# A hybrid HGRN2 / retention layer step: query pads inside the value stage, one gate moved across a round's border, two small groups of matmuls in 64-column tiles

## What is computed

```
xn = RMSNorm(h); hq, hf, hi, hg, rq, rk, rv, rg, ga, gb = split(xn @ w_in)
# branch A: 8 heads, state 64x64, chunk by chunk
f = lb + (1 - lb) * sigmoid(hf)
S_t = diag(f_t) S_{t-1} + (1 - f_t) i_t^T ;  o_t = S_t^T silu(q_t)
a_hg = head_rmsnorm(o_hg) * silu(hg)
# branch B: 4 heads of 128, rotary q and k, decay gamma_h
a_r = head_rmsnorm(retention(q_r, k_r, rv)) * silu(rg)
mixed = sigmoid(ga) * (a_hg @ w_br_hg) + sigmoid(gb) * (a_r @ w_br_ret)
h = h + mixed @ w_out ; h = h + ConvFFN(RMSNorm(h)) ; h = h + ple gate ; y = RMSNorm(h)
```

## Time and profile before

| what | value |
|---|---|
| median of 3 runs | 937.52 us (937.37 to 937.79) |
| the profiled execution, its own time | 936.62 us |
| its span, first to last instruction | 934.8 us |
| PE busy | 911.3 us, 97% of the span |
| DVE, ACT, POOL busy | 56%, 42%, 25% |
| granted TensorE clock | 0.995 |

### The profile page before, as it was taken

The page is one execution under the profiler, slowest core; times in us unless marked ns, Lnnn a source line. Parts: engine busy times, 40 slices in busy tenths (PEclk is TensorE's granted clock), DMA queues, the critical chain, the costliest instruction groups (busy, mean ns, idle before and its releaser), DMA issues. The chain is left out here.

```text
span 934.8 us, 20997 instructions
## 1 busy us (share of the span) xinstructions
PE 911.3 (97%) x7950; PEld 896.8 (96%) x7950; DVE 523.9 (56%) x613; ACT 388.7 (42%) x518; POOL 236.0 (25%) x289
## 2 busy tenths in 40 slices
PE   6999999999999999999999999999999999999996
PEld 5999988999999999999999999999999999999995
DVE  6432267777655655566566655555556433435653
ACT  7323356446345544323344444444443322213433
POOL 0006076777211010002631111111111021212341
PEclk9999999999999999999999999999999999999998
DMA  6333533233254434633323333333333333332212
GB/s 223 93 91 90 180 92 80 79 90 79 79 137 112 127 97 135 199 117 99 90 68 91 90 90 90 91 90 94 94 94 105 102 93 93 93 90 70 81 54 91
DMA packets 176471, 94.72 MB, mean 101 GB/s; under 512 B 17888, under 2 KB 174960, under 8 KB 176016
## 3 DMA queue, kind: packets, MB, share of 16 engines
q1 hardware_dynamic: 149698, 80.61, 29.0%
q10 hardware_dynamic: 26736, 13.60, 5.5%
HBM read 86.25 MB, written 8.03 MB: 101 GB/s over the span
## 5 line engine op out<-in xcount | busy, mean ns | idle before, releaser
L832 ACT ACTIVATE whi<-raw 128x1024 fp32r<-128x1024 f32 (+2 forms) x132 | 146.9, 1113 | 351.0 <-PE acc L486 350.2
L1169 DVE TENSOR_TENSOR wlo<-raw,whi 128x1024 fp32r<-128x1024 f32 (+2 forms) x132 | 195.7, 1482 | 172.3 <-ACT whi L832 172.3
L486 PE MATMUL acc<-xah,whi 128*128 128x260 f32 x896 | 186.9, 290 | 0.0
L486 PE MATMUL acc<-xah,wlo 128*128 128x260 f32 x896 | 180.2, 283 | 0.0
L486 PE MATMUL acc<-xal,whi 128*128 128x260 f32 x896 | 179.7, 282 | 0.0
L486 PE MATMUL acc<-xbh,whi 128*128 128x260 f32 x816 | 165.3, 284 | 0.8 <-issue 0.8
L486 PE MATMUL acc<-xbh,wlo 128*128 128x260 f32 x816 | 164.4, 283 | 0.0
L486 PE MATMUL acc<-xbl,whi 128*128 128x260 f32 x816 | 164.2, 283 | 0.0
L486 PEld LDWEIGHTS acc<-xah,whi 128*128 128x128 f32 x896 | 137.9, 189 | 3.3 <-issue 1.9
L486 PEld LDWEIGHTS acc<-xal,whi 128*128 128x128 f32 x896 | 137.9, 188 | 0.0
L486 PEld LDWEIGHTS acc<-xah,wlo 128*128 128x128 f32 x896 | 137.8, 188 | 0.0
(11 more groups left out here) (287 smaller groups left out, 1183.4 us busy)
## 6 DMA issues: line engine op xcount, KB each, us to landing
raw<-in_w_in SPq DMA_DIRECT2D x96, 256.0 KB, 3.1
raw<-in_w_up SPq DMA_DIRECT2D x88, 256.0 KB, 3.1
raw<-in_w_down SPq DMA_DIRECT2D x16, 384.0 KB, 3.3
raw<-in_w_down SPq DMA_DIRECT2D x16, 320.0 KB, 3.7
raw<-in_w_out SPq DMA_DIRECT2D x16, 256.0 KB, 3.0
raw<-in_w_ple_gate SPq DMA_DIRECT2D x8, 512.0 KB, 3.8
x_transposed<-xstg SPq DMA_DIRECT2D x1, 2080.0 KB, 7.5
hT<-x_transposed ACTq DMA_DIRECT2D x1, 2080.0 KB, 7.9
```

The lines of the kernel that those rows point to most:

```text
L486: mm = pe.matmul(sums[:, b, 0:HT], wt[slot][:, w], xx[:, c, b * HT:(b + 1) * HT], start=first and i == 0 and q == 0, stop=last and i == n ...
L832: act.activation(whi[k % 2][:, 0:n], raw[k % 2][:, 0:n], ACT.Copy).then_inc(hi_ready, 1)
L1169: dve.tensor_tensor(wlo[k % 2][:, 0:n], raw[k % 2][:, 0:n], whi[k % 2][:, 0:n].bitcast(fp), SUB).then_inc(lo_ready, 1)
```

## The change

Six edits. (1) ACT's loop over section V is written out, and the pads of the levels 0 to 3 of the first round are made inside its second half, two levels after each of the first two units. (2) At the end of a B round ACT makes `branch_hi` before the sigmoid. (3) DVE makes the gate `grt` of a round not at its end but in the next round, between `merge(0)` and `merge(1)`; for this the first round is written out ahead of the loop, and the last gate stands behind it. (4) L578 and L691 become twice as many matmuls of 64 weight columns, one for each half of the output partitions. (5) In a C round the copy and the squares of the samples' outputs stand ahead of the low weight part. (6) The small sums of squares stand behind four chunks instead of five.

```diff
--- before.py
+++ after.py
@@ -575,7 +575,9 @@
                 taken()
                 if use == 3:
                     for c in range(4):
-                        pe.matmul(lvb[:, 1, 2 * c:2 + 2 * c], qk[:, c, :], headsel, start=True, stop=True)
+                        for r in range(2):
+                            rows = slice(64 * r, 64 * r + 64)
+                            pe.matmul(lvb[rows, 1, 2 * c:2 + 2 * c], qk[:, c, rows], headsel, start=True, stop=True)
                 for l in levels:
                     for c in range(4):
                         out = lvb[:, l % 2, c * 128:(c + 1) * 128].rearrange("s (two t) -> s two t", two=2)
@@ -688,16 +690,18 @@
                 pe.wait_ge(smp_staged, it + 5)
                 pe.wait_ge(rsm_ready, it + 1)
                 for b in range(NS):
-                    mm = pe.matmul(mb[:, b:b + 1], rsm[:, b, :], qs8[:, b:b + 1], start=True, stop=True)
+                    for r in range(2):
+                        rows = slice(64 * r, 64 * r + 64)
+                        mm = pe.matmul(mb[rows, b:b + 1], rsm[:, b, rows], qs8[:, b:b + 1], start=True, stop=True)
                 mm.then_inc(misc_full, 1)
 
-                product("C", 3, it, 1, 3, range(5), 0, xah, xal, last=False)
+                product("C", 3, it, 1, 3, range(4), 0, xah, xal, last=False)
 
                 pe.wait_ge(smp_sq, it + 1)
                 wait_misc(M_C, 3, it, 4)
                 pe.matmul(mb[:, 0:8], blk64, sqs[:, 0:8], start=True, stop=True)
                 pe.matmul(mb[:, 8:16], ones128[:], sqs[:, 8:16], start=True, stop=True).then_inc(misc_full, 1)
-                product("C", 3, it, 1, 3, range(5, 8), 5, xah, xal, first=False, wait_unit=False)
+                product("C", 3, it, 1, 3, range(4, 8), 4, xah, xal, first=False, wait_unit=False)
 
             pe.wait_ge(ah_lo, 17)
             with pe.Fori(0, 2) as it:
@@ -881,24 +885,6 @@
                     else:
                         act.wait_ge(f_done, it * 2 + (k // 2 + 1))
                         act.activation(two(sgf[:]), ps2(1), ACT.Sigmoid).then_inc(acc_free[1], 1)
-            with act.Fori(0, 2) as it:
-                for k in range(4):
-                    done("V", k, it)
-                    ahead("V", k, it)
-                    if k % 2 == 0:
-
-                        act.wait_ge(v_full, it * 4 + (k + 1))
-                        act.activation(two(hiT[:]), ps2(0), ACT.Copy).then_inc(acc_free[0], 1)
-                    else:
-                        act.activation(two(sg[1][:]), ps2(1), ACT.Sigmoid).then_inc(sig_ready, 1)
-                        act.wait_ge(v_full, it * 4 + (k + 1))
-                        taken()
-                        cols = bass.ds(it * 256 + 128 * (k // 2), 128)
-                        act.activation(vhg[:, :, cols], m4(lvb[:, 0, :]), ACT.Copy).then_inc(v_taken, 1)
-                        act.wait_ge(v_full, it * 4 + (k + 2))
-                        taken()
-                        act.activation(v8h[:, cols], lvb[0:NS, 1, 0:128], ACT.Copy).then_inc(v_taken, 1)
-
             def chunk(t, c):
                 return t[:, :, bass.ds(c * CH, CH)]
 
@@ -923,11 +909,31 @@
                     ins = act.activation(dst, src, ACT.Copy)
                 ins.then_inc(zq_ready, 1)
 
+            for it in range(2):
+                for k in range(4):
+                    done("V", k, it)
+                    ahead("V", k, it)
+                    if k % 2 == 0:
+
+                        act.wait_ge(v_full, it * 4 + (k + 1))
+                        act.activation(two(hiT[:]), ps2(0), ACT.Copy).then_inc(acc_free[0], 1)
+                    else:
+                        act.activation(two(sg[1][:]), ps2(1), ACT.Sigmoid).then_inc(sig_ready, 1)
+                        act.wait_ge(v_full, it * 4 + (k + 1))
+                        taken()
+                        cols = slice(it * 256 + 128 * (k // 2), it * 256 + 128 * (k // 2) + 128)
+                        act.activation(vhg[:, :, cols], m4(lvb[:, 0, :]), ACT.Copy).then_inc(v_taken, 1)
+                        act.wait_ge(v_full, it * 4 + (k + 2))
+                        taken()
+                        act.activation(v8h[:, cols], lvb[0:NS, 1, 0:128], ACT.Copy).then_inc(v_taken, 1)
+                    if it == 1 and k < 2:
+
+                        act.wait_ge(set_up, 7)
+                        for l in (2 * k, 2 * k + 1):
+                            pad_queries(l, 0)
+
             act.wait_ge(v_taken, 9)
             act.dma_start(vs_dram[0], v8h[:]).then_inc(vs_stored, 16)
-            act.wait_ge(set_up, 7)
-            for l in range(4):
-                pad_queries(l, 0)
 
             def hgrn_chunk(it, last=False):
                 act.wait_ge(misc_full, it * 4 + (M_B - 2))
@@ -980,8 +986,8 @@
                         pad_queries(l, it + 1)
                 done("B", 3, it)
                 ahead("B", 3, it, "C" if last else None)
+                branch_hi(ahh, it, 0)
                 act.activation(two(sg[1][:]), ps2(3), ACT.Sigmoid).then_inc(sig_ready, 1)
-                branch_hi(ahh, it, 0)
 
             with act.Fori(0, 3) as it:
                 hgrn_chunk(it)
@@ -1300,9 +1306,16 @@
                 dve.wait_ge(ah_hi, it + (n + 1))
                 dve.tensor_tensor(chunk(t_lo, it), m4(ot[:]), chunk(t_hi, it).bitcast(fp), SUB).then_inc(ah_lo, 1)
 
-            with dve.Fori(0, 4) as it:
-                step.loop(it, 6)
+            def last_gate(it):
+                dve.wait_ge(sig_ready, it + 9)
+                dve.scalar_tensor_tensor(two(grt[:, it, :]), ps2(3), vc[:, bass.ds(it + 44, 1)],
+                                         two(sg[1][:]), MUL, MUL).then_inc(acc_free[1], 1)
+
+            def hgrn_chunk(it, before=None):
                 merge(0, it)
+                if before is not None:
+
+                    last_gate(before)
                 merge(1, it)
                 done("B", 0, it)
                 ahead("B", 0, it)
@@ -1344,14 +1357,19 @@
 
                 done("B", 3, it)
                 ahead("B", 3, it)
-                dve.wait_ge(sig_ready, it + 9)
-                dve.scalar_tensor_tensor(two(grt[:, it, :]), ps2(3), vc[:, bass.ds(it + 44, 1)],
-                                         two(sg[1][:]), MUL, MUL).then_inc(acc_free[1], 1)
                 dve.wait_ge(misc_full, it * 4 + (M_B + 4))
                 taken()
                 dve.tensor_copy(qT[:, it, NT:TT], mb[:, 0:NS]).then_inc(misc_free, 1)
                 branch_lo(ahl, ahh, it, 0)
-            step.end(4)
+
+            step.loop(0, 6)
+            hgrn_chunk(0)
+            step.end(1)
+            with dve.Fori(0, 3) as it:
+                step.loop(it, 6)
+                hgrn_chunk(it + 1, before=it)
+            step.end(3)
+            last_gate(3)
 
             dve.wait_ge(misc_free, M_C)
             with dve.Fori(0, 4) as it:
@@ -1376,8 +1394,6 @@
                 dve.scalar_tensor_tensor(grown, grown, gam[:, bass.ds(it, 1)], vb[:], MUL, ADD).then_inc(rsm_ready, 1)
                 dve.wait_ge(misc_free, it * 4 + (M_C + 2))
                 gate_outputs(grt, it, 4, per=3)
-                done("C", 2, it)
-                ahead("C", 2, it)
                 dve.wait_ge(misc_full, it * 4 + (M_C + 3))
                 taken()
                 dve.tensor_copy(qr[:, it, NT:TT], mb[:, 0:NS]).then_inc(misc_free, 1)
@@ -1387,6 +1403,8 @@
                 cols = qT[:, it, NT:TT], qr[:, it, NT:TT]
                 dve.tensor_tensor(sqs[:, 0:8], cols[0], cols[0], MUL)
                 dve.tensor_tensor(sqs[:, 8:16], cols[1], cols[1], MUL).then_inc(smp_sq, 1)
+                done("C", 2, it)
+                ahead("C", 2, it)
                 branch_lo(arl, arh, it, 4)
                 dve.wait_ge(misc_free, it * 4 + (M_C + 4))
                 step(dve.reciprocal(rss[:], rss[:]))
```

## The result

The changed kernel takes 932.53 us (median of 4 runs, 932.39 to 932.88), the kernel before 937.44 (4 runs, 936.73 to 937.79): ratio 0.9947, 95% interval [0.9935, 0.9959]. It is 4.9 us faster, where 6.4 were forecast. The profiled execution took 932.57 us, its span is 930.8, that is 4.0 less than before.

A forecast was written before the change was run, and what follows sets the result against it. PE, busy 97% of the span, was taken as the bound; 1.63 + 1.32 + 1.04 + 1.65 + 0.74 = 6.38 us off 937.52 gave 931.1 us, own range 930.3 to 932.3, wider range 929.8 to 934.1.

The forecast's parts named there:

- Pads in the value stage: Round 0, first scores: ACT makes the padded queries earlier, inside section V, so PE's wait for them goes; gain 1.63 us.
- The gate across the border: B rounds 1 to 3: PE's 2.1 us of `sfull` waits go, 0.26 comes back three times at `scores(2)`; gain 1.32 us.
- Cost nothing: Moved gate and earlier `branch_hi`: `acc[1]` is freed in time and the sigmoid is wanted later, so no loss.
- 64-column tiles, L691: Sample outputs in C rounds: 1.93 us falls to 1.38 as in L648, 0.55 a round, 1.65 over the first three.
- 64-column tiles, L578: Diagonal block in B rounds: 1.12 us falls to 0.86, a gain of 0.26 a round, 1.04 in four.
- C rounds: First three rounds gain 0.55 each, 1.65; in the last, earlier squares and sums start section D 0.74 us earlier.
- margin of 0.4 at the small sums: C rounds: DVE's squares end at 373.4, PE reaches the sums at 373.8; if late, PE pays in each of 4 rounds.
- the start of section D some 6.4 us earlier than 378.50: Sign that the forecast is right: section D's start in PE's timeline moves up by some 6.4 us.
- the rival whose merges stay late: B rounds: DVE's merges stay late, so only tiles, pads and the D start count; gain 5.1, 932.5 us; chance 0.10.
- tiles that give nothing: L578 and L691: draining and loading eat the 64-column tiles' savings; gain 3.5, 934.0 us; chance 0.11.
- the count of instructions: L578 and L691: each half costs a full instruction, 0.106 us, adding 10.3 us; slower, 944.9 us; chance 0.04.
- All waits go: B rounds: the 0.26 us waits go too, and L578 gives 1.4; gain 7.5, 930.0 us; chance 0.07.

## Why the prediction was right, and where not

**Pads in the value stage:** right in mechanism and size, 1.62 against 1.63.

**The gate across the border:** right. All three `sfull` waits go, the short `zq` waits take their place as round 0 had shown. Alone it gives 1.45 in the B stretch; the sum had 1.32. The kernel with only the C rounds edited has 137.06 in place of 137.35, so this stretch scatters by some 0.3 where the `sfull` waits are. "Cost nothing" held too: no wait on `grt`.

**64-column tiles, L691:** right; 0.58 a block and 1.68 over three rounds against 1.65. The changes of mode cost no more than the 0.09 that L648's row had shown.

**64-column tiles, L578:** the step that failed. "The difference is 0.26, in four rounds 1.04": the block does get 0.30 shorter (0.82 for 1.12; its own 16 instructions take 0.49, where 0.6 were named as the sign), but only the last round keeps it. The sum counted time off PE's queue as gain, since the list of PE's waits showed none behind it. It should have asked for the slack of the next thing that PE waits for: at the head squares PE already lost 0.2 to 0.3 in each of the rounds 0 to 2 to DVE's state update, and DVE's way there starts ahead of the block. 0.7 of the forecast's excess is this.

**C rounds:** right, 2.39 against 2.39. The squares were ready 0.5 ahead of PE (370.02 and 370.53). But the parts are not independent as I had them: without the earlier squares the tiles give 0.41 a round. The forecast's margin of 0.4 at the small sums came from these.

**The sum against the median:** the forecast took its savings off the median as if all else stayed. It didn't: PE's half-speed stretch at the start was longer in the profiles of the changed kernel. With PE kept busy there, the two kernels are 5.85 apart, near the 5.66 of the marks. The two profiles themselves were not alike either: the one of the kernel before is 0.8 below its median (936.62 and 937.44), the one of the changed kernel at its median (932.57 and 932.53). So a usual execution of the kernel before has some lateness as well, which would leave 0.8 of the 1.6 between the two; that all of it lies at the start isn't shown. For the same reason the sign "the start of section D some 6.4 us earlier than 378.50" did not come: it is 374.44, 4.1 earlier, 0.7 short by the block above and 1.6 by the start. Why the start is later with the change, or whether five profiles on each side are only chance, stays open; the text of the program that runs there is the same. One profile does not tell how the start scatters, and the range held no term for it.

932.53 lies inside the stated range of 929.8 to 934.1 and 0.2 above the forecast's own 930.3 to 932.3.

The time is also just that of the rival whose merges stay late (932.5), and its mechanism did not happen: all `sfull` waits are gone. The time alone would have pointed to it. The rivals: tiles that give nothing, late merges and the count of instructions all fall by the marks. "All waits go" falls too; it needed two more edits.

## What to carry to other kernels

A saving on the busiest engine is kept only up to the slack of what it waits for next; read that slack as the step between the starts of two pieces against the same step elsewhere, since a loss of 0.2 us showed in no line of PE's waits, only among those of its weight loads. Measure between marks that lie on both sides of an edit; edits of 1 us could not be told apart by the time of the whole, and could to 0.03 us by marks, unless a wait stood between them. An order of parts that costs nothing alone (the squares behind the weight part) can be what another part needs.

## What the hardware showed unexpectedly

PE's first products ran at the lower of its two levels for up to some 3.5 us (0.43 us a step instead of 0.24) in eight profiles and at the upper one in two, those of the kernel before and of the pads alone. The idle time ahead doesn't part them: it was 1.74 to 2.04 us in the eight, 2.04 and 1.52 in the two. Ten filler instructions in that idle time (1.28 us together), and ten at the very start, had it at the upper level in all three profiles that had them. The same level change shows at the end, where ten small matmuls behind the last idle times took 1.28 us in some profiles and 1.8 to 1.9 in others, and the whole end 1.0 to 1.2 us more. Between the two, stretches without a changing wait repeat to 0.02 us: from the start of D to section F 95.26 to 95.28 us in twelve of the thirteen profiles.
